# Twelve sublayers on one core: modulation sums, gain rows and PSUM banks in a new order

## The reference

```python
def _ffn_sublayer(h, mod, g_pre, g_post, w_in, w_out):
    shift, scale, gate = mod
    u = _modulate(_rmsnorm(h, g_pre), shift, scale)
    a, b = jnp.split(u @ w_in, 2, axis=-1)
    y = (jax.nn.silu(a) * b) @ w_out
    return h + MACARON_W * gate * _rmsnorm(y, g_post)
...
        mx = (silu_c @ ada_w[i] + ada_b[i]).reshape(B, N_MOD, 1, D)
        mc = (silu_cc @ ada_w[i] + ada_b[i]).reshape(N_MOD, D)
```

## Time and profile before

| | |
|---|---|
| median of 3 runs | 2852.43 us (2845.12 to 2854.97) |
| the profiled execution | 2847.95 us, its span 2846.2 us |
| PE busy | 2757.5 us, 97% |
| DVE busy | 2053.7 us, 72% |
| ACT busy | 1607.9 us, 56% |
| POOL busy | 138.7 us, 5% |
| read from memory | 559.17 MB, 197 GB/s over the span |

### The profile page before, as it was taken

How to read it: one execution, slowest core, us unless ns; L and a number is a source line. 1 busy time by engine, 2 the same in 40 slices (tenths; PEclk the granted TensorE clock), 3 DMA queues, 4 the chain that set the end, 5 groups by cost and what they waited for, 6 DMA issues and landing times.

```text
span 2846.2 us, 37779 instructions
## 1 busy us (share of the span) xinstructions
PE 2757.5 (97%) x14816; PEld 2329.6 (82%) x14816; DVE 2053.7 (72%) x2655; ACT 1607.9 (56%) x2431; POOL 138.7 (5%) x140
## 2 busy tenths in 40 slices
PE   6999999989999999999999999999899999998999
PEld 5888888768888888888887788887688888896887
DVE  7879887777888898886536565665666565696664
ACT  5455555676555555555646654554855454476553
POOL 0000000000000000000040000000000000194000
PEclk9999999999999999999999999999999999999999
DMA  8667784206677787985552355554355565440553
GB/s 339 217 236 272 243 256 169 105 27 238 224 274 252 219 298 265 296 252 192 178 208 98 125 194 196 195 190 166 133 201 192 178 207 193 176 168 11 210 184 132
DMA packets 100561, 562.72 MB, mean 198 GB/s; under 512 B 20256, under 2 KB 20768, under 8 KB 43936
## 3 DMA queue, kind: packets, MB, share of 16 engines
q1 hardware_dynamic: 100384, 560.30, 56.8%
HBM read 559.17 MB, written 1.09 MB: 197 GB/s over the span
## 4 chain that ended last, share of the span: by engine, by line
PE 72%; DVE 10%; ACT 5%; issue 5%; DMA 4%; POOL 3%; SPq 0%; DVEq 0%; ACTq 0%; POOLq 0%
PE banks L867 19%; PE banks L873 10%; PE banks L368 9%; PE banks L369 9%; PE banks L1041 7%; PE banks L373 3%; PE banks L375 3%; PE banks L374 3%; DVE ada_terms L449 3%; DVE w_rest L352 3%; ACT w_high L342 2%; POOL od_glu L2374 2%; PE banks L841 2%; POOL normed L2370 1%; DMA w_raw<-in_w_ffn_in 1%
## 5 line engine op out<-in xcount | busy, mean ns | idle before, releaser
L352 DVE TENSOR_TENSOR w_rest<-w_raw,w_high 128x2048 fp32r<-128x2048 f32 x426 | 975.2, 2291 | 495.4 <-ACT w_high L342 494.5
L342 ACT ACTIVATE w_high<-w_raw 128x2048 fp32r<-128x2048 f32 x426 | 811.1, 1908 | 336.3 <-PE banks L1041 161.8
L867 PE MATMUL banks<-u_parts,w_high 128*128 128x512 f32 x3200 | 764.3, 391 | 2.2 <-DVE post_term L557 2.2
L867 PEld LDWEIGHTS banks<-u_parts,w_high 128*128 128x128 f32 x3200 | 588.2, 188 | 116.9 <-issue 2.5
L873 PEld LDWEIGHTS banks<-u_parts,w_rest 128*128 128x128 f32 x3200 | 410.2, 191 | 16.6 <-DVE w_rest L352 1.1
L873 PE MATMUL banks<-u_parts,w_rest 128*128 128x256 f32 x3200 | 415.2, 283 | 0.6 <-DVE w_rest L352 0.6
L368 PE MATMUL banks<-w_high,gated_high 128*128 128x512 f32 x968 | 378.9, 391 | 1.7 <-DVE gated L947 1.7
L369 PE MATMUL banks<-w_high,gated_rest 128*128 128x512 f32 x968 | 377.5, 390 | 0.0
L449 DVE CUSTOM_DVE_ANT_0 ada_terms<-ada_tiles,cond_rows 128x1024 f32<-128x1024 f32 x224 | 273.7, 1222 | 12.0 <-DMA ada_tiles<-in_w_ada 6.9
L1041 PE MATMUL banks<-w_rest,gated_high 128*128 128x512 f32 x968 | 258.9, 389 | 0.1
L368 PEld LDWEIGHTS banks<-w_high,gated_high 128*128 128x128 f32 x968 | 182.3, 188 | 39.3 <-issue 2.1
(11 more groups left out here) (307 smaller groups left out, 3334.6 us busy)
## 6 DMA issues: line engine op xcount, KB each, us to landing
w_raw<-in_w_ffn_in SPq DMA_DIRECT2D x242, 1024.0 KB, 5.0
w_raw<-in_w_ffn_out SPq DMA_DIRECT2D x121, 1024.0 KB, 5.0
ada_tiles<-in_w_ada SPq DMA_DIRECT2D x128, 512.0 KB, 5.0
w_raw<-in_w_mix SPq DMA_DIRECT2D x54, 1024.0 KB, 5.0
w_raw<-in_w_mix_out SPq DMA_DIRECT2D x22, 1024.0 KB, 4.9
ada_first<-in_w_ada SPq DMA_DIRECT2D x7, 1024.0 KB, 14.9
post_gain_row<-post_mod SPq DMA_DIRECT2D x10, 512.0 KB, 5.9
na_bias<-in_na_bias SPq DMA_DIRECT2D x1, 4096.0 KB, 14.1
```

The source lines that it names most:

```text
L342: act.activation(w_high(g)[:, 0:n], raw[:, g % RING, 0:n], ACT.Copy).then_inc(w_hi_ready, 1)
L352: nc.vector.tensor_tensor(w_rest(g)[:, 0:n], raw[:, g % RING, 0:n], w_high(g)[:, 0:n].bitcast(F32), ALU.subtract).then_inc(w_lo_ready, 1)
L867: pe.matmul(ps[n].rearrange("p (a n) -> p a n", a=2), hi[:, w], u[:, c, :, kt], start=kt == 0, stop=False)
```

## The change

It has four parts. (1) In the pipelined passes `post_scales` stands ahead of the first rest of block f = 0 rather than behind it. (2) In the out phases the modulation sums of step 0 are done in step 1, those of steps 1 to 6 after the step's `stat_dve` or `part_dve`, and those of steps 7 to 10 ahead of the step's rest. The code does this in all pipelined feed-forward passes. (3) The row of a gate is fetched no earlier than two slots after its store (slots 32 and 114 in place of 30 and 112), and rows are asked for ahead of whatever else `between_slots` does at that slot. (4) Banks: outputs of stages 2 and 3 are in banks 6, 7 and 4, 5, with gates in 0 to 3 and 4 to 7 in turn; outputs of stages 5, 8 and 11 lie in banks 4, 5 and 1, 3; stages 6 and 9 (`behind_ffn`) have another order of input banks. The last block's gates then share no bank with an output, and the wait of the second token tile on the last gate sum goes.

```diff
@@ y_pair @@
-            return pairs[{(1, 0): [0, 1], (1, 1): [3, 2], (4, 0): [0, 1], (7, 0): [0, 1], (10, 0): [3, 2]}
-                         .get((s, c), [2, 1] if exposed(s) else [3, 1])[tt]]
+            if exposed(s) and s in FFNS and not behind_ffn(s):
+                return banks[:, 1:4:2] if tt else pairs[2]
+            return pairs[{(0, 0): [3, 1], (0, 1): [3, 1], (1, 0): [0, 1], (4, 0): [0, 1], (6, 0): [2, 1], (7, 0): [0, 1],
+                          (9, 0): [2, 1]}.get((s, c), [3, 2])[tt]]
@@ banks @@
+        def behind_ffn(s):
+            return s - 1 in FFNS
         def in_bank(s, f, tt):
-            return tt + 2 * (f % 2) if not exposed(s) else 2 * tt + f % 2
+            return tt + 2 * (f % 2) if not exposed(s) or behind_ffn(s) else 2 * tt + f % 2
@@ gate_banks @@
             if exposed(s):
+                if behind_ffn(s):
+                    return ([6, 7, 0, 1], [4, 5, 2, 3])[f % 2]
                 return ([6, 7, 0, 2], [4, 5, 1, 3])[f % 2]
-            if (s, c) == (2, 0):
-                return ([0, 1, 2, 3], [4, 5, 6, 7])[f % 2]
-            return ([0, 1, 4, 5], [2, 3, 6, 7])[f % 2]
+            if s == 0:
+                return ([0, 1, 4, 5], [2, 3, 6, 7])[f % 2]
+            return ([0, 1, 2, 3], [4, 5, 6, 7])[f % 2]
@@ ffn_out_pe @@
-                if k == 0 and tt == 1:
-                    if by_token(s, c, NF - 1):
-                        pe.wait_ge(gate_done, b0 + 2 * NF)
-                    elif exposed(s) or (s, c) == (2, 0):
-                        pe.wait_ge(in_summed, sums_before(s, c, NF))
+                if k == 0 and tt == 1 and by_token(s, c, NF - 1):
+                    pe.wait_ge(gate_done, b0 + 2 * NF)
@@ ffn_dve, in phase @@
+                if f == 0 and not exposed(s):
+                    post_scales(*ends_beside(s, c), 1)
                 rests(g0 + 2 * f + LEAD)
                 if f == 0 and not exposed(s):
-                    post_scales(*ends_beside(s, c), 1)
                     post_add(*ends_beside(s, c), 1)
@@ ffn_dve, out phase @@
+                if j > 6:
+                    sums_at(g1 + j)
                 rests(split_upto(s, c, j))
                 if j == 0:
                     glo_dve(s, c, NF - 1)
-                sums_at(g1 + j)
                 if not exposed(s):
                     o = starts_beside(s, c)
...
                     if j == 6:
                         part_dve(*o, 1)
+                if j == 1:
+                    sums_at(g1)
+                if 0 < j <= 6:
+                    sums_at(g1 + j)
@@ SP @@
-            gain_after.setdefault(max(g + AHEAD, store_spot.get(s, 0)), []).append((s, c))
+            gain_after.setdefault(max(g + AHEAD, store_spot.get(s, -2) + 2), []).append((s, c))
...
         def between_slots(sp, g):
+            for s, c in gain_after.get(g, []):
+                load_post_gain(sp, s, c)
...
             if g in store_after:
                 store_post_mod(sp, store_after[g])
-            for s, c in gain_after.get(g, []):
-                load_post_gain(sp, s, c)
```

## The result

The changed kernel took 2859.68 us (median of 7 runs, 2855.64 to 2864.91), the kernel before 2852.43 us (7 runs beside it, 2845.12 to 2854.97). (The table under "Time and profile before" speaks of 3 runs; its median and range are those of these 7.) The ratio is 1.0031, with a 95% interval of 1.0020 to 1.0042: slower by some 9 us. The profiled execution of the changed kernel took 2855.64 us itself, 7.7 more than that of before.

A forecast was written before the change was run, and what follows sets the result against it. PE, busy 97% of the span, was taken as the bound, with DVE a close second in the out phases. Terms -10.4 + 4.6 + 15.5 = +9.7 us on 2847.95 gave 2857.7, plus 4.5 for the median: 2862 us, range 2849 to 2870.

The forecast's parts named there:

- second wait: Stage 3's first out phase: PE waits 7.1 us (6 to 8) for the rest of slot 10.
- The new waits of stages 0 and 2: Slot 10's rest comes late in both passes of stages 0 and 2: 4 x 1.15 = 4.6 us (2 to 7.6).
- the circle: Stage 3's first pass: tile refill queues behind weights awaiting a rest, which follows sums needing the tile; rests 10.0 us apart.
- The removed waits: Seven PE waits near the edited code go, 8.78 us, plus 1.6 us of clock: 10.4 us (at least 6.0).
- (a): Scales ahead of the rest at f=0 start about 2.2 us earlier; waits of 0.87 and 1.31 us go.
- (b): Stage 1's context-pass row is fetched earlier, DVE runs some 4 us earlier; the 0.65 us wait goes.
- (c): Gain rows fetched two slots after their store: 4 us of stage 2's delay saved, the 1.75 us wait goes.
- (d): Norm's steps ahead of the sums: waits of 0.25 and 2.97 us go, and 1.6 us of lost clock.
- (e): The 0.98 us wait at 413.25, ending on a rest behind two sums, goes as those sums move earlier.
- rival 3: Store's delay is not removed, (c) gives nothing: +2 us, 2864; forecast and this rival together have chance 0.60.
- The first (small waits): New waits are small, as DVE is on time and tiles land in 4.8 us: 2851 to 2858; chance 0.27.
- The second: Sums ahead of rests 9 to 11 fit into DVE's idle time, no new wait: 2843 to 2846; chance 0.13.

The follow-up runs named there:

- norm's order alone: Kernel before with first scales ahead of the rest and sums of steps 0 to 6 behind the norm's steps; steps 7 to 10 as before: 2850.76 us, 1.0015.
- tail's order alone: Kernel before with only the sums of steps 7 to 10 put ahead of the rest of their step: 2857.13 us, 1.0029.
- one phase here: Kernel before with gain rows moved and sums of steps 1 to 6 behind the norm's steps only in stage 3's first out phase: 2841.86 us, 0.9971.
- tail put back: Changed kernel with the sums of steps 7 to 10 behind the rest of their step again: 2845.28 us, 0.9988 of the kernel before.
- norm's order taken back: Changed kernel without the norm's order; tail's order, banks and rows stay changed: 2854.58 us, 1.0018 of the kernel before.

## Why the prediction was right

**Time, range, sign.** It gave 2862 us in 2849 to 2870 with 0.60 on slower; 2859.68 us and a ratio of 1.0031 came. In the profiled executions it gave +9.7 us, and +7.7 came. Its terms were all of stages 0 to 3, and there +11.0 came, read at matmul 6300; the later stages, where it had nothing, gave back 3.3. That the whole came within 2 us of the forecast is thus in part luck. Two terms do not follow from their own working: 0.5 + 6.2 + 1.2 + 2.2 is 10.1, which less 2.7 makes a second wait of 7.4 and not 7.1, and rest 10 of out2c comes 1.06 us late and not 1.15, so 4.2 for the four. The two slips nearly cancel.

**The new waits of stages 0 and 2: right.** Predicted 4 x 1.15 = 4.6 us; 2.00 + 1.06 + 1.06 + 1.33 = 5.45 came. On out2c the rest of slot 10 ends at 1035.0 against 1036.1 worked out, in a pass that turns 1.5 us earlier. That all four are alike was almost right: out0x waits twice as long in this execution, where DVE also stands 1.07 us for a tile, in the slots behind the store of stage 0. The kernel with tiles asked for earlier has the same code there and waits 1.25.

**Stage 3: the circle was right, its split was not.** Predicted 0.7 + 6.1 + 7.1 and 1.6 for the clock, 15.5 us. Measured 0.35 + 5.97 + 4.18, and the clock took 2.8 us between the waits and some 1.5 behind them: 14.8. With 5.45 for the other waits, 0.42 left at 409 us and 10.4 removed that makes +10.3, beside the 11.0 at matmul 6300. The turn takes 9.7 us against the 10.0 of the sum. The mis-sized terms are the second wait and the clock, and they are one: PE at the half clock wants the rest of slot 10 later by what it loses. The low clock of the earlier trace rows should have been put on the stretch between the two waits. The kernel with earlier tiles shows that the second wait hangs on SP's order: it is gone with DVE's order untouched.

**The removed waits: the list was right, the reasons were not.** All seven went. But I gave each to one edit, and the single parts show that most have two sufficient ones: those at 233, 361, 679 and 682 us go with the rows alone and with the norm's order alone, and the first three of them with the tail's order alone too. So (a) and (b) count the same microseconds. What I sized as 2.4 us for (b) and (c) is 4.6 to 6.3 us when measured, and (a) with (d), sized at 5.4 + 1.6, cost 3.7 to 4.3 us instead. Here lies the step that failed: for the sums put behind the norm's steps I counted 0.7 us of small waits, and otherwise only what they add to the tail's long waits. But they are owed even where the tail stands as before: in the kernel with the norm's order alone PE pays at 216, 413, 1190 and 1225 us (1.08, 2.08 in place of 0.98, 0.58 and 3.28), with a low clock behind two of these. The sum came out since in the changed kernel the largest part of the debt, at slots 9 and 10 of stage 3, was in my count under the tail. (e) was half right: 0.42 us is left of 0.98.

**The store's delay (c), rival 3.** Issue of stage 2's store and the next start of ACT on weights, in the changed kernel, beside the earlier trace rows:

```profile
771.01 2.51 SPq L487 DMA_DIRECT2D post_mod<-post_scale  x2
...
789.06 1.92 ACT L342 ACTIVATE w_high<-w_raw 128x2048 fp32r<-128x2048 f32 x1 [3.77 <-DMA w_raw<-in_w_ffn_out]
```

That is 18.1 us from store to start, against 19.9 before and the 15.8 that I took: 1.8 us won where I had 4. Yet with the rows moved alone 798 us had no wait, so it was enough there, and rival 3's 2 us did not come. The Trainium skill's "DMA: Bandwidth & Descriptors", section "Queues, rings and completion order", says that descriptors of a ring are consumed in ring order; in kind the 18.1 us agree: these weights were issued 5.1 us behind the store, which SP does not wait for, and took 12.9 us to land, where the median of weight loads is 5.0. But ring order is not all of it: the load issued 0.4 us ahead of the store, at 770.64, took 12.0 us (12.6 with the rows alone). No run here measures the store by itself. The row itself was right: issued at 660.01, it is in place when DVE comes at 670.12, where the earlier trace rows had 5.19 us of idle time.

**Rivals.** The first (small waits) is refuted by 5.97 and 4.18 us, and its reason, faster tiles, shows only in 5.8 us for the tile of the circle where I took 6.2; the second wait is short because of the clock. The second asked whether sums ahead of rests fit into DVE's idle time: in out0c, out2x and out2c they do when the tail's order is changed alone, and they do not once the norm's order has pushed step 6's sums behind the split. In stage 3 they do not either way.

**Banks of stages 5 to 11** were costed at nothing; banks alone gave 0.9996 and, from matmul 6300 on, 0.4 us more than before.

## What to carry to other kernels

Work that is put off on an engine busy 92% of the time, as DVE is here, is not moved but owed: look for the rest or load that it meets next, and put it off only in the phase whose wait is worth more than that (one phase here gave as much as all). When a wait goes, find out by single edits which one did it; here two or three edits each sufficed for the same waits, and one of them cost 4 us elsewhere. Where a program has a long untouched part behind the change, compare the same instruction at the end of the changed part: here the untouched part moved by 3 us from one execution to the next, as much as a whole part of the change is worth. On a ring of buffers, follow the freed buffer through the queue that refills it: if the refill stands behind a load that waits for the very work that waits for the refill, the stage runs at the pace of that circle.

## What was not expected of the hardware

A loss of clock can hide part of a later wait: with 12 matmuls at 0.50 of the full clock the second wait was 4.18 us, not the 7.0 that 9.7 - 2.7 would give.

Equal waits do not always cost the same clock. With the norm's order alone the granted clock was 0.62 over the 4 us behind the 2.08 us wait at 413 us, which is some 1.6 us lost; in the changed kernel with its tail put back the wait at that place is 2.08 us as well, and the clock stayed full:

```profile
413.10:417.10 4.00, 4.00 (x22) 3.41 (x23) 3.22 (x8) 3.92 (x8) 0.00 (x0) 1.00 0.73 259
```

Nor does a longer wait always cost more. Over 4 us the clock was 0.59 behind 2.97 us (kernel before), 0.57 behind the 4.18 us at 1178 us (rows alone) and 0.58 behind 6.65 us (norm's order taken back); between the two long waits of the changed kernel it was 0.50 throughout. Behind the 2.00 us wait at 216 us the four L1049 matmuls took 1.20 us, near the 1.07 of undisturbed ones; behind 5.97 us they took 2.07.

Weights are late around a store of a gate even when SP does not wait for it: in the changed kernel the load issued 5.1 us behind the store took 12.9 us, and the one issued 0.4 us ahead of it 12.0.
